# One of four early modulation blocks moved from TensorE to the vector engine, through slot 3

## The reference

```python
def adaln(cond, w, b):
    m = jax.nn.silu(cond) @ w + b
    return jnp.split(m, 3, axis=-1)
...
shift, scale, gate = adaln(c, ada_w[i], ada_b[i])
h = modulate(rms_norm(x, norm_g[i]), shift[:, None], scale[:, None])
shift_c, scale_c, gate_c = adaln(c_ctx, ada_w[i], ada_b[i])
hc = modulate(rms_norm(ctx, norm_g[i]), shift_c, scale_c)
```

## Time and profile before

| | us |
|---|---|
| median of 3 runs | 3159.15 |
| lowest and highest | 3153.58, 3159.34 |
| the profiled execution | 3150.54 |
| its span | 3148.5 |
| PE busy in the span | 2959.1 (94%) |
| DVE busy | 771.8 (25%) |
| ACT busy | 389.2 (12%) |

### The profile page before, as it was taken

One profiled execution on the slowest core, in us unless ns is written; L12 is line 12 of the kernel. 1 busy time (PEld: TensorE's weight loads), 2 busy tenths in 40 slices (PEclk: granted clock), 3 DMA queues, 4 the chain that ended last, 5 costly groups with the idle time before them and its releaser, 6 DMA issues. The chain is left out here.

```text
span 3148.5 us, 30098 instructions
## 1 busy us (share of the span) xinstructions
PE 2959.1 (94%) x12188; PEld 2238.2 (71%) x12188; DVE 771.8 (25%) x1503; ACT 389.2 (12%) x747; POOL 48.3 (2%) x68
## 2 busy tenths in 40 slices
PE   7999999999998999999997998999999899999999
PEld 1376766677666655555555887888888788878878
DVE  1342334233333244444452001101010200001110
ACT  0111111101111122222220001000000011111110
POOL 0000000000000000000000000000000000000000
PEclk9999999999999999999998998999999999999999
DMA  9764555445552233333323444555544354434432
GB/s 354 270 219 139 176 163 166 151 160 165 158 164 95 72 96 93 93 93 94 94 96 99 146 135 146 155 146 153 158 149 146 109 159 134 131 112 137 139 110 77
DMA packets 379149, 444.85 MB, mean 141 GB/s; under 512 B 20308, under 2 KB 351560, under 8 KB 378312
## 3 DMA queue, kind: packets, MB, share of 16 engines
q1 hardware_dynamic: 353200, 361.15, 37.6%
q0 software_dynamic: 17408, 67.11, 6.2%
q10 hardware_dynamic: 8472, 15.58, 1.3%
HBM read 439.56 MB, written 4.26 MB: 141 GB/s over the span
## 5 line engine op out<-in xcount | busy, mean ns | idle before, releaser
L458 PE MATMUL bank<-hT,w 128*128 128x256 f32 (+1 forms) x6144 | 1631.4, 427 | 6.0 <-ACT hT L933 4.5
L458 PEld LDWEIGHTS bank<-hT,w 128*128 128x128 f32 x6144 | 1175.6, 192 | 437.4 <-issue 310.0
L458 PE MATMUL bank<-w,hT 128*128 128x256 f32 (+1 forms) x2176 | 463.4, 374 | 0.0
L458 PE MATMUL bank<-yT,w 128*128 128x256 f32 x2048 | 450.6, 383 | 5.6 <-DVE yT L1671 4.1
L458 PEld LDWEIGHTS bank<-w,hT 128*128 128x128 f32 x2176 | 404.3, 191 | 60.9 <-issue 8.6
L458 PEld LDWEIGHTS bank<-yT,w 128*128 128x128 f32 x2048 | 393.2, 192 | 61.2 <-DVE yT L1671 4.5
L933 ACT ACTIVATE work<-bank 128x512 f32<-128x512 f32 (+3 forms) x292 | 153.8, 556 | 1717.8 <-PE bank L458 1712.8
L458 PE MATMUL bank<-work 128*128 128x256 f32 (+2 forms) x400 | 132.7, 456 | 91.7 <-DVE work L1407 53.8
L1422 DVE SCALAR_TENSOR_TENSOR work<-xT,silc,work 128x512 f32<-128x512 f32 x240 | 180.5, 752 | 39.9 <-DMA xT<-in_ada_w 31.9
L458 PEld LDWEIGHTS bank<-work 128*128 128x128 f32 x400 | 79.2, 211 | 118.2 <-issue 67.0
L933 ACT ACTIVATE work<-work 128x512 f32<-128x512 f32 (+4 forms) x243 | 135.0, 556 | 194.2 <-DVE work L1487 128.0
(11 more groups left out here) (105 smaller groups left out, 844.8 us busy)
## 6 DMA issues: line engine op xcount, KB each, us to landing
w<-in_na_ssd_w_in SPq DMA_DIRECT2D x48, 2048.0 KB, 8.5
xT<-in_ada_w POOLq DMA_DIRECT2D x64, 1024.0 KB, 5.8
w<-in_sc_w_in SPq DMA_DIRECT2D x32, 2048.0 KB, 10.6
w<-in_w_in SPq DMA_DIRECT2D x32, 2048.0 KB, 10.6
w<-in_ada_w SPq DMA_DIRECT2D x16, 2048.0 KB, 10.2
w<-in_na_ssd_w_out SPq DMA_DIRECT2D x16, 2048.0 KB, 8.6
w<-in_na_ssd_w_in SPq DMA_DIRECT2D x16, 1024.0 KB, 7.4
w<-in_sc_w_out SPq DMA_DIRECT2D x8, 2048.0 KB, 8.3
```

Source lines behind the costliest of these rows:

```text
L458: return nc.tensor.matmul(dst, lhsT, rhs, start=start, stop=stop, skip_group_check=free)
```

## The change

One block (columns 3072 to 4095, the last quarter) is no longer PE's. Its four tiles all pass through slot 3, and the DVE multiplies each 128x1024 piece with the condition's scalar per row and adds it up in a new SBUF buffer `eacc` (128 x 2 x 1024), for c and for c_ctx: eight passes a tile. At the end PE adds `eacc` over the partitions with 16 products by two columns of ones, into columns 64 to 95 of bank 0. The twelve tiles of the other three blocks (numbered u = 0 to 11) pass through slots 0 to 2. x's transposes now follow tiles 5 to 8, and DVE's four parts are written between its other work. SP's list is: t = 0, 1, 2: slots 0, 1, 2, 3; t = 3: slot 3, then 0, 1, 2. The bias add becomes two instructions.

```diff
-        for b in range(EARLY):
-            for q in range(SLOTS):
-                wait(sp, ada_used, (b - 1) * SLOTS + q + 1)
-                sp.dma_start(early(q), w_ada[0][:, 4 * q:4 * q + 4, b * 4 * TILE:(b + 1) * 4 * TILE]).then_inc(
-                    w_loaded[q], 16)
+        def early_tile(s, b, q):
+            sp.dma_start(early(s), w_ada[0][:, 4 * q:4 * q + 4, b * 4 * TILE:(b + 1) * 4 * TILE]).then_inc(
+                w_loaded[s], 16)
+
+        for t in range(4):
+            for s in ((0, 1, 2, 3) if t < 3 else (3, 0, 1, 2)):
+                if s < 3:
+                    wait(sp, ada_used, 3 * (t - 1) + s + 1)
+                    early_tile(s, (3 * t + s) // 4, (3 * t + s) % 4)
+                else:
+                    wait(sp, early_taken, t)
+                    early_tile(3, 3, t)
...
-                    return sp.wait_ge(ada_used, (EARLY - 1) * SLOTS + s + 1)
+                    return sp.wait_ge(ada_used, 10 + s) if s < 3 else sp.wait_ge(early_taken, 4)
...
+        for u in range(12):
+            b, q, s = u // 4, u % 4, u % 3
             rows_of = (bank[3][:, :], bank[4][:, :]) if b % 2 == 0 else (wide[:, 0:512], wide[:, 512:1024])
...
+            if q == 0:
+                wait(pe, ada_row, 2 * (b - 1))
+            pe.wait_ge(w_loaded[s], 16 * (u // 3 + 1))
...
+            last.then_inc(ada_used, 1)
+            if 5 <= u < 9:
+                if u == 5:
+                    pe.wait_ge(x_in, 64)
+                for kc in range(4 * (u - 5), 4 * (u - 4)):
+                    x_turned(kc)
+            if u == 8:
+                early_turn(0)
                 pe.wait_ge(params_in, 16 * 17)
                 for n in range(1, 4):
                     last = tr(bank[2][:, n * P:(n + 1) * P], prm[:, n, :])
                 last.then_inc(cols_pe, 1)
+            if u == 10:
+                early_turn(1)
+        pe.wait_ge(cols_dve, 2)
+        norm_sums(0, T + TC)
+        pe.wait_ge(early_taken, 4)
+        for ch in range(8):
+            for k in range(2):
+                n = 64 + 4 * ch + 2 * k
+                last = mm(bank[0][:, n:n + 2], eacc[:, k, ch * P:(ch + 1) * P], ONES[:, 0:2])
+        last.then_inc(ada_turned, 1)
+        early_turn(2)
...
+        def early_part(q):
+            dve.wait_ge(w_loaded[3], 16 * (q + 1))
+            tile = w3.rearrange("p (a b) -> p a b", a=4)
+            for kc in range(4):
+                for k in range(2):
+                    s = sil[:, 16 * k + 4 * q + kc:16 * k + 4 * q + kc + 1]
+                    if q + kc == 0:
+                        last = v.tensor_scalar(eacc[:, k, :], tile[:, kc, :], s, None, ALU.mult)
+                    else:
+                        last = v.scalar_tensor_tensor(out=eacc[:, k, :], in0=tile[:, kc, :], scalar=s, in1=eacc[:, k, :],
+                                                      op0=ALU.mult, op1=ALU.add)
+                if kc < 3:
+                    link(last)
+            last.then_inc(early_taken, 1)
+            dve.wait_ge(early_taken, q + 1)
+
+        early_part(0)
         early_rows(0)
+        early_part(1)
         for kc in range(DC):
             dve.wait_ge(xt_pe, kc + 1)
...
         v.tensor_copy(colp[:, P:4 * P], bank[2][:, P:4 * P]).then_inc(cols_dve, 1)
         early_rows(1)
+        early_part(2)
         norm_sum_squares(0, 2, T + TC)
+        early_part(3)
         early_rows(2)
-        early_rows(3)
```

More of the change, by code:

```diff
@@ L188, in program @@
     arow = L(2, 4 * TILE)
+    eacc = L(2, 4 * TILE)
     L = Lay(work, WORK)
@@ L279, in program @@
     late_in = [sem(f"late_in{r}") for r in range(2)]
-    late_taken, late_sum, x_saved, x_back = (sem(n) for n in ("late_taken", "late_sum", "x_saved", "x_back"))
+    early_taken, late_taken, late_sum, x_saved, x_back = (sem(n) for n in ("early_taken", "late_taken", "late_sum", "x_saved", "x_back"))
     consts_in, params_zeroed, c_in, params_in, x_in, ssd_in = (
@@ L518, in early_turn @@
             last.then_inc(ada_turned, 1)
-        for b in range(EARLY):
+        for u in range(12):
+            b, q, s = u // 4, u % 4, u % 3
             rows_of = (bank[3][:, :], bank[4][:, :]) if b % 2 == 0 else (wide[:, 0:512], wide[:, 512:1024])
[L522 to L536, removed]
+            if q == 0:
+                wait(pe, ada_row, 2 * (b - 1))
+            pe.wait_ge(w_loaded[s], 16 * (u // 3 + 1))
+            tile = w[s][:, :, :].rearrange("p a b -> p (a b)").rearrange("p (a b) -> p a b", a=4)
+            for kc in range(4):
+                for half in range(2):
+                    last = mm(rows_of[half][0:2, :], pair[:, 4 * q + kc, :],
+                              tile[:, kc, half * 512:(half + 1) * 512], q + kc == 0, q + kc == 6)
+            last.then_inc(ada_used, 1)
[6 more added lines that the diff above has]
+                early_turn(0)
                 pe.wait_ge(params_in, 16 * 17)
@@ L1362, in _ @@
         bias = colp[:, ds(COLUMN["ada_b0"], 32)].unsqueeze(2).broadcast_to([P, 32, 2])
-        v.tensor_tensor(mod[:, 0, 0:32, :], bank[0][:, 0:64].rearrange("p (a b) -> p a b", b=2), bias,
+        v.tensor_tensor(mod[:, 0, 24:32, :], bank[0][:, 64:96].rearrange("p (a b d) -> p a b d", b=2, d=2)[:, :, :, 0:1].rearrange("p a b d -> p a (b d)"),
+                        bias[:, 24:32, :], ALU.add)
+        v.tensor_tensor(mod[:, 0, 0:24, :], bank[0][:, 0:48].rearrange("p (a b) -> p a b", b=2), bias[:, 0:24, :],
                         ALU.add).then_inc(mod_ready, 1)
```

## The result

The kernel became slower, as forecast: 3161.75 us is the median of 19 executions (3158.88 to 3168.5), against 3152.97 for 19 of the kernel before (3150.47 to 3159.34). The ratio is 1.0028, with a 95% interval of 1.0021 to 1.0035, so +8.8 us where +10.7 was forecast. The forecast's absolute figure, 3169, was 7 us too high, mostly because the first three runs of the kernel before lay high in its spread: over 19 runs its median is 6.2 us lower. The changed kernel's times lie in two groups, nine of them at 3159 to 3160 and eight at 3164 to 3165, and its median is the single one between; so +8.8 stands between about +6.4 and +11.4, and that it comes within 2 us of the forecast is in part luck.

A forecast was written before the change was run, and what follows sets the result against it. TensorE bounds the early stage: -25.8 us for the moved block, then +1.9, +4.9, +2.0, +24.6, +2.7 and +0.2 give +10.5, stated as +10.7: 3161 against the profiled run, about 3169 against the median; range 3157 to 3178.

The forecast's parts named there:

- What leaves and what comes: PE's early stage: one block (-27.6 us) and its early turn (-1.9) go, 32 short records come (+3.7); sum -25.8.
- Wait A: PE's fourth tile: its load into slot 0 lands at 41.1, PE is ready at 39.2; +1.9 us.
- DVE's price: Eight 128x1024 passes per tile cost DVE 10.1 us, the first tile 9.1; bounds 6.0 and 12.2.
- Wait B: Among x's transposes: PE stops until DVE's second part ends at 67.4 and copies begin; +4.9 us, plus 2.0 for the clock.
- Wait C: Before PE's tenth tile: SP issues its load only after DVE's third part ends at 112.7; landing 125.3, +24.6 us.
- The half clock behind it: PE's tenth tile, after the long stop: the granted clock has fallen, so its 16 records cost +2.7 us.
- Sum: Early stage up to PE's last early turn, ending near 159.4: terms add to +10.5 us, stated as +10.7.
- Rival 1: Tenth tile not held up if DVE's third part ends by 102: 27.3 us vanish, -16.6 in all, 3143; 5%.
- counted as hidden: DVE's fourth part, ending at 137, and its 14.12 us reduction lie beside PE's last tiles, ending at 150.6; no cost.

The follow-up runs named there:

- Experiment 2: Changed kernel with DVE's passes of parts two to four over 64 of their 1024 columns; 3148.7 us, ratio 0.999 to the kernel before.
- experiment 1: Changed kernel with only SP's fourth round reordered, slots 0, 1, 2, 3 in place of 3, 0, 1, 2; 3156.38 us, ratio 1.0008 to the kernel before.
- Experiment 3: Changed kernel with DVE's part three ahead of the copies of x's columns 8 to 15, SP's list kept; 3149.8 us, ratio 0.9992.
- experiment 7: Kernel of experiment 6 with SP's fourth round through slots 3, 0, 1, 2 as in the changed kernel; 3142.33 us, ratio 0.9973.
- second execution: The changed kernel run and profiled once more, nothing edited; 3159.17 us.
- experiment 6: Changed kernel with DVE's parts cut between copies, part four before the reduction, SP's order 0, 1, 3, 2, PE's norm sum behind the 32 products; 3134.0 us, ratio 0.994.
- experiment 4: Changed kernel with its 16 sums by two columns of ones done twice, 64 records in place of 32; 3171.5 us, ratio 1.0055.
- experiment 8: Kernel of experiment 6 with the first early turn behind the tenth tile: 3134.59 us, ratio 0.995; beside it that kernel unedited: 3133.91 us, 0.9945.

## Why the prediction was right

**What leaves and what comes.** 64 records and a turn left; the 32 that came cost 3.7 us at full clock, as forecast, but 2.8 more in the profiled execution (48 records in 8.38 against 5.62). This is the one term that the sum lacked. I had taken the late sums' 1.84 us per 16 as the rate of a string of 48, and had looked for a falling clock only in waits. A string of 16 is over in 1.84 us, and the falls seen here came 2.1 and 5.3 us behind the start of the 48.

**Wait A.** 1.91 us, 1.9 forecast.

**DVE's price.** 10.03 us per tile, 10.1 forecast, and 9.0 for the first, 9.1 forecast: the slope between 256 and 512 columns carried over to 1024. The passes are 1281 and 749 ns:

```profile
L1368 DVE SCALAR_TENSOR_TENSOR work<-w,work 128x1024 f32<-128x1024 f32 x30 | 37.2, 1281 | 8.4 <-DMA w<-in_ada_w 8.0
L1366 DVE TENSOR_SCALAR work<-w,work 128x1024 f32<-128x1024 f32 x2 | 1.4, 749 | 21.6 <-DMA w<-in_ada_w 21.6
```

**Wait B.** Slot 3's second tile landed at 57.8 (57.3 forecast) and the part ended at 67.8 (67.4). PE came to its seventh tile at 70.58, 69.5 forecast: half from the landing, half from transposes that already ran at half clock. Without the stop it would have been 62.06 + 2.8 = 64.9, so +5.7 where 4.9 was forecast. The tile itself took 1.5 us more (8.56 for 7.03): in all 7.2, against 4.9 + 2.0 = 6.9. Experiment 2 shows both go when the part is short.

**Wait C.** 24.40 us, 24.6 forecast; part three ended at 115.4, 12.6 us before the tile was there, as computed. That the step is right in its cause too, experiments 1, 3 and 7 show: SP's list and DVE's list each had the slow one in front. The half clock behind it cost 15.69 - 13.90 = 1.8, where I had taken 2.7 from the start of the kernel.

**Sum.** Forecast for the early stage +10.7, in the profile +13.0, in the second execution 158.29 - 148.84 = +9.5, in the medians +8.8. The forecast lies between the two executions; most of their difference is the clock at the short records (2.8 of 3.6 us up to "na"). In the first profile the errors lean against each other: the half clock behind wait C was put 0.9 us too high, the short records 2.8 too low. Rival 1 did not come about, as its 5% said, but its price was wrong as well. It took away wait C and its clock, 27.3 us, as if nothing else then held PE. Experiment 3 meets its condition (part three ends at 92.9, before 102) and the kernel comes out 0.08% under the kernel before, some 2.5 us and not 16.6; experiment 1 has no stop before the tenth tile either and gains nothing. In both PE then waits for the DVE's fourth part, which the prediction had counted as hidden; it was hidden only behind wait C. The 18 us of experiment 6 needed more than that.

## What to carry to other kernels

When work is moved to an idle engine, follow every in-order list that the move couples: here a load that one engine needed stood in a third engine's list behind a slot that the idle engine freed late, because its own list had other work in front. Idle time of an engine is only usable where its list puts it: cut the moved work to the length of the pauses (7 us here) and put loads in the order in which their slots come free. Then look again for what ends last: here it was the vector engine's fourth part and 14 us reduction, and TensorE's coming 1.0 us sooner changed nothing. A stop also hides other work: what it covered has to be priced again before its removal is counted as gain.

## What the runs showed of the hardware

TensorE's granted clock falls not only while the engine waits. In the string of 48 products by two columns, which has no pause in it, it went from 1.00 to 0.50 (2.4 to 1.2 GHz) in both executions of the changed kernel, at 155.6 us in one and 157.9 in the other, and in experiments 2 and 4 too. A record then took 0.20 to 0.22 us instead of 0.117. How early it falls differs between executions of one program, by 2.8 us of time here, and what decides that is not settled.

Among the transposes and the 19 short records behind them it fell in the three executions that had a wait of 1.07 us there (experiments 6, 7 and 8), and in none of the kernel before, the changed kernel and experiments 1 and 2, with 0.41 us. Experiment 3, with 0.41 us but a stop of 3.59 us one tile earlier, fell at the string's end. With a tile of dense matmuls between the strings it held over two tiles, in one profile, and fell at the next string.

Times of one kernel lie in groups some 5 us apart (3159 and 3164, 3151 and 3156, 3142 and 3148). For the first pair two profiles lay 2.8 us to the string of 48; for the others there is no second profile, and the same cause is not shown. Where the change does nothing, as near 1010 us in experiment 1, the clock can still move microseconds. Whether the shift of the early stage or chance decides there is not settled.
